# Streaming-encoder trunk on one core: families, merge gates and output projection issue each product as two of 256 columns

## What is computed

```python
mod = silu(c) @ ada_w + ada_b                 # shift, scale, gate
h = rms_norm(x, norm_w) * (1 + scale) + shift # 4096 x 1024
p = h @ w_in                                  # the families below
gq, gk, gv, gz, glr, hq, hf, hi, hz, mg = split(p)
o_g = gated linear attention (gq, gk, gv, decay from glr), normed, * silu(gz)
o_h = HGRN2 recurrence (hq, hf, hi), normed, * silu(hz)
g_a, g_b = split(sigmoid(mg + merge_b))       # merge gates
m = g_a * (o_g @ w_up_gla) + g_b * (o_h @ w_up_hgrn)
out = rms_norm(x + gate * (m @ w_out), final_norm_w)
```

## Time and profile before

| | |
|---|---|
| median of 3 timed executions | 2898.24 us (2897.74 to 2898.29) |
| the profiled execution's own time | 2897.05 us |
| its span in the trace | 2895.3 us |
| TensorE busy | 2863.4 us, 14662 MATMULs, 14662 weight loads |
| VectorE busy | 1522.8 us |
| ScalarE busy | 1265.2 us |

### The profile page before, as it was taken

How to read it: one execution, slowest core, us unless ns; L and a number is a source line. 1 busy time by engine, 2 the same in 40 slices (tenths; PEclk the granted TensorE clock), 3 DMA queues, 4 the chain that set the end, 5 groups by cost and what they waited for, 6 DMA issues and landing times.

```text
span 2895.3 us, 38295 instructions
## 1 busy us (share of the span) xinstructions
PE 2863.4 (99%) x14662; PEld 2344.6 (81%) x14662; DVE 1522.8 (53%) x2004; ACT 1265.2 (44%) x1659; POOL 168.8 (6%) x295
## 2 busy tenths in 40 slices
PE   7999999999999999999999999999999999999998
PEld 4878888788887888888888888888888788887887
DVE  6555455544556445564554635546355463644644
ACT  3643336433463334633446433464335533355322
POOL 1010000100001000010000100001000010000100
PEclk9999999999999999999999999999999999999999
DMA  8223442233322343224432243322433224342232
GB/s 326 88 81 119 134 142 90 78 131 131 133 94 75 131 136 129 87 80 138 138 126 87 74 152 126 125 88 74 154 123 131 83 74 159 109 137 83 81 124 73
DMA packets 89950, 336.21 MB, mean 116 GB/s; under 512 B 9808, under 2 KB 10000, under 8 KB 88208
## 3 DMA queue, kind: packets, MB, share of 16 engines
q1 hardware_dynamic: 89744, 333.45, 34.8%
HBM read 316.63 MB, written 16.78 MB: 115 GB/s over the span
## 4 chain that ended last, share of the span: by engine, by line
PE 98%; DMA 1%; DVE 0%; ACT 0%; SPq 0%; POOL 0%; issue 0%; POOLq 0%; DVEq 0%; ACTq 0%
PE A L1024 46%; PE F L1035 33%; PE A L1084 12%; PE R L1120 1%; PE F L1147 1%; PE A L1162 1%; PE R L1203 1%; PE F L1141 1%; DMA ada_w<-in_ada 1%; PE R L1113 1%; PE R L1147 0%; PE R L1187 0%; PE R L1186 0%; PE R L1162 0%; PE R L971 0%; PE A L982 0%
## 5 line engine op out<-in xcount | busy, mean ns | idle before, releaser
L662 DVE TENSOR_TENSOR w_lo<-w_raw,w_hi 128x1024 fp32r<-128x1024 f32 (+1 forms) x480 | 588.4, 1226 | 1059.9 <-ACT w_hi L451 1056.3
L451 ACT ACTIVATE w_hi<-w_raw 128x1024 fp32r<-128x1024 f32 (+1 forms) x480 | 507.4, 1057 | 752.8 <-PE A L1024 479.8
L1024 PE MATMUL A<-w_hi,h_hi 128*128 128x512 f32 (+1 forms) x1536 | 582.5, 379 | 0.1
L1024 PE MATMUL A<-w_lo,h_hi 128*128 128x512 f32 (+1 forms) x1536 | 572.9, 373 | 0.0
L1024 PE MATMUL A<-w_hi,h_lo 128*128 128x512 f32 (+1 forms) x1536 | 572.6, 373 | 0.0
L1035 PE MATMUL F<-h_hi,w_hi 128*128 128x512 f32 x1408 | 553.9, 393 | 0.0
L1035 PE MATMUL F<-h_lo,w_hi 128*128 128x512 f32 x1408 | 548.3, 389 | 0.0
L1035 PE MATMUL F<-h_hi,w_lo 128*128 128x512 f32 x1408 | 548.2, 389 | 0.0
L1024 PEld LDWEIGHTS A<-w_hi,h_hi 128*128 128x128 f32 x1536 | 288.3, 188 | 61.2 <-issue 9.4
L1024 PEld LDWEIGHTS A<-w_hi,h_lo 128*128 128x128 f32 x1536 | 288.5, 188 | 51.5
L1024 PEld LDWEIGHTS A<-w_lo,h_hi 128*128 128x128 f32 x1536 | 288.6, 188 | 47.5 <-issue 0.2
(11 more groups left out here) (188 smaller groups left out, 2832.3 us busy)
## 6 DMA issues: line engine op xcount, KB each, us to landing
w_raw<-in_w_stream SPq DMA_DIRECT2D x464, 512.0 KB, 3.5
xy<-in_x SPq DMA_DIRECT2D x8, 2048.0 KB, 8.6
result<-xy SPq DMA_DIRECT2D x32, 512.0 KB, 3.5
xf<-in_xt SPq DMA_DIRECT2D x30, 512.0 KB, 4.3
xn<-in_x SPq DMA_DIRECT2D x28, 512.0 KB, 5.1
ada_w<-in_ada SPq DMA_DIRECT2D x12, 1024.0 KB, 19.9
w_raw<-in_w_stream SPq DMA_DIRECT2D x16, 544.0 KB, 6.0
xy<-in_x SPq DMA_DIRECT2D x4, 512.0 KB, 13.8
```

Source lines behind the costliest of these rows:

```text
L451: AF(w_hi[:, s % RING, 0:n], w_raw[:, s % RAW, 0:n], ACT.Copy).then_inc(w_hi_done.sem, 1)
L662: V.tensor_tensor(w_lo[:, s % RING, 0:n], w_raw[:, s % RAW, 0:n], w_hi[:, s % RING, 0:n].bitcast(fp32), ALU.subtract).then_inc(w_split.sem, 1)
L1024: last = mm(A[t][:, 0:width], src[ia][:, k, t * P:(t + 1) * P], w_[iw][:, s % RING, kk * width:(kk + 1) * width], start=(k == 0 and n == 0 ...
```

## The change

Wherever `token_major` has a width of 512, and in all of `feature_major`, the products run over columns 0 to 255 first and then over columns 256 to 511, with the loop over the halves outside the loop over the pieces. Each half repeats all weight loads. Only the very first product of a bank has the start flag. The 272-column products, the up projection and the hosted products stay as they are.

```diff
                 for t in range(NT):
                     if part == 0:
                         pe.wait_ge(free.sem, free.at(b, free_n[t]))
-                    for kk in range(k_per):
-                        k = part * k_per + kk
-                        for n, (ia, iw) in enumerate(PASSES):
-                            last = mm(A[t][:, 0:width], src[ia][:, k, t * P:(t + 1) * P],
-                                      w_[iw][:, s % RING, kk * width:(kk + 1) * width],
-                                      start=(k == 0 and n == 0), stop=(k == KT - 1 and n == 2))
+                    for c0, c1_ in ((0, 256), (256, 512)) if width == 512 else ((0, width),):
+                        for kk in range(k_per):
+                            k = part * k_per + kk
+                            for n, (ia, iw) in enumerate(PASSES):
+                                last = mm(A[t][:, c0:c1_], src[ia][:, k, t * P:(t + 1) * P],
+                                          w_[iw][:, s % RING, kk * width + c0:kk * width + c1_],
+                                          start=(k == 0 and n == 0 and c0 == 0), stop=(k == KT - 1 and n == 2),
+                                          skip_group_check=True)
...
             def feature_major(b, s, dst):
-                for k in range(KT):
-                    for n, (iw, ia) in enumerate(PASSES):
-                        last = mm(dst[:, :], w_[iw][:, s % RING, k * P:(k + 1) * P], h_[ia][:, k, :],
-                                  start=(k == 0 and n == 0), stop=(k == KT - 1 and n == 2))
+                for fr in (slice(0, 256), slice(256, 512)):
+                    for k in range(KT):
+                        for n, (iw, ia) in enumerate(PASSES):
+                            last = mm(dst[:, fr], w_[iw][:, s % RING, k * P:(k + 1) * P], h_[ia][:, k, fr],
+                                      start=(k == 0 and n == 0 and fr.start == 0), stop=(k == KT - 1 and n == 2),
+                                      skip_group_check=True)
                 last.then_inc(slot_done.sem, 1)
```

## The result

The changed kernel takes 3032.6 us (median of 4, 3029.4 to 3035.2) against 2898.3 (2897.7 to 2898.9): a ratio of 1.046, 95% interval 1.0445 to 1.0481, 134 us slower. The forecast was slower, 2980 us with a range of 2950 to 3035, so the direction and the range held, and the likeliest value was 53 us short.

What follows compares the result with a forecast made beforehand. The prediction took TensorE to bound the kernel: 2897.05 us for the profiled execution plus 80 for slower split products made 2977, 2978 with the median's 1.2 above the profiled run, rounded up to 2980, range 2950 to 3035.

Steps and rivals of the forecast that it cites:

- What bounds the kernel: Whole kernel: TensorE bounds it, 98% of the chain, so longer products go straight into the time.
- the 1820 forecast: Weight loads: 9600 added at 0.19 us each would raise their busy time by about 1820 us.
- Why a product of 256 columns costs more than half: Split products: a 128-column load, 0.11 us, nearly fills its 0.114 us cover, so load and stream touch.
- The rival of the load that hides whole: Split products: each added load hides under its predecessor's 256 columns; 2898 to 2907 us, chance 0.12.
- The 24 us estimated from it: Split products: by the skill's columns over 2.4 GHz plus 2.5 ns, the split adds 24 us, giving 2922.
- (a): Split products take the tri products' pace, 117.5 ns: 8.3 ns more for each of 9600, 80 us.
- addresses as what could make it wrong: Split products: pace may differ between token_major and feature_major or between passes, unseen in tri rows; no size given.
- The rival of the fixed cost: Split products: a fixed cost each whatever the width, 119.3 ns at 256 columns; 114 us, 3012 us, chance 0.25.
- 256 columns no faster than 272: Split products: the load sets 126.0 ns, so two cost 252.0; 243 us more, 3141 us, chance 0.05.
- The rest, costed at nothing: Slot starts, semaphores, queued work on ScalarE and VectorE, and adding up in one bank: no added time.
- The rival on the fetching of instructions: TensorE's 400 split slots: a stall of some 0.1 us each adds 40 us, about 3020 us, chance 0.03.

Runs made afterwards that it cites:

- e1: Changed kernel with feature_major put back whole, so only token_major's 512-column products are split: 2979.1 us, ratio 1.028.
- e2: Changed kernel with token_major put back whole, so only feature_major's products are split: 2953.1 us, ratio 1.019.
- e8: Changed kernel with feature_major loading only 64 of 128 columns of each weight piece, leaving out half the rows: 2976.5 us in one execution.
- e12: Changed kernel with w_hi and w_lo moved 64 bytes on in memory, nothing else different: 2971.9 us, ratio 1.0252.
- e11: Kernel before plus eleven runs of 48 products, loaded or moving piece of h shifted in memory: 117.9 to 120 ns at 256 columns; total time not given.
- e7: Kernel before plus ten runs of 48 products ahead of tri, varying operands and widths: 113.3 to 120 ns at 256 columns; total time not given.
- e5: Changed kernel with the products split at column 384 instead of 256: 3485.9 us, ratio 1.203.
- e3: Changed kernel with slot 59, the last of each block, left whole: 3017.3 us, ratio 1.0411.
- e10: Kernel before plus ten other runs of 48 products, with fixed or changing weights and 64 or 96 loaded columns; total time not given.
- e13: Kernel before, products whole, with w_hi and w_lo moved 64 bytes on in memory: 2944.2 us, ratio 1.016.
- e9: Kernel before with only slot 59, the last of each block, split: 2913.2 us, ratio 1.0054.

## Why the prediction was right, and where it was off

*What bounds the kernel.* Right. 9600 products were split (e1 and e2 add up to the change), and what each got longer went straight into the time. The weight loads' records, added up, rose from 2643 to 4524 us, near the 1820 forecast, but that isn't what a page calls busy: there overlapping loads are merged, and the rise is 515 us.

*Why a product of 256 columns costs more than half.* The mechanism held, in part. With half the load it runs at 113.4 ns (e8), which is the half of 226.7, and the cost is then nothing; with the whole load it is 120.0. But a load as long as its cover isn't enough by itself: in e12 the whole load of 128 columns costs nothing in the merge gates (113.4), so the cost takes the long load and this placement together. The rival of the load that hides whole is refuted for these operands where they lie, and comes true in that other placement for part of the slots. What goes on between load and stream at a multiple of 256 bytes no run shows. The Trainium skill ("TensorE: Matmul & The Clock Gate", section "Back-to-back issue gap"), which the prediction set beside this rival, gives its columns over 2.4 GHz plus 2.5 ns for a product by itself and not for a stream of them. The 24 us estimated from it compare with 128 here.

*The value taken, (a), 117.5 ns.* This is the term that was mis-sized: 120.0 ns, so 128 us in place of 80. "Because width, loaded columns and type are the same" was not enough. `tri` lies 192 bytes off a multiple of 256 and the pieces of the change on one, and e11 gives 117.9 and 120.0 for just this difference. The prediction named addresses as what could make it wrong, and took no other value for it.

*The rival of the fixed cost* gave 119.3 ns and 3012 us, closer than my own value. As a number it holds from 256 to 512 columns (120.0, 146.7, 173.3, 226.7). As a mechanism it fails: half a load brings 113.4 at 256 columns (e8), and below that stands a floor of 112 ns (e7) which took e5 to 3486 us.

*256 columns no faster than 272.* Refuted, 120 against 126.

*"The rest, costed at nothing."* The starts of slots were right to within 0.06 us each. What was missing is the loop's branch, some 10 us. The rival on the fetching of instructions put a stall at each of 400 slots; it sits at 6 places, 1.6 to 2.0 us beyond a product's pace each. I had looked at how fast instructions are issued and not at what covers the fetch behind a branch.

*The sum as it came out:* 2898 + 128 + 10 + 2 - 7 = 3031, for 3032.6 measured. The 2 is the up projection.

What stays open: why 320 and 384 columns take their length plus 13.3 ns whether 64 or 128 columns are loaded, why 512 columns take 230.0 with 64 loaded and 226.7 with 128, what picks 113.3 or 117.8 ns where load and stream aren't a multiple of 256 bytes apart, and why 512 columns are slower there.

## What to carry to other kernels

Where a weight load is nearly as long as the product that covers it, halving the columns need not be free even though stream and load both fit: here 6.7 ns for each product of 256 columns, and 4.6% of the whole with the gaps. A price taken from another product of the same shape was 2% off here and made a third of the loss go missing, since the place of the operands in memory moves it (113 to 120 ns at the same width). And the products at the end of TensorE's loop are what covers the fetch behind the branch: with the last slot left whole (e3) what was left of each gap is 0.26 us or nothing. Keep long instructions last.

## What the runs showed of the hardware that was not expected

- Load and stream together depend on where they lie to one another in memory: 120.0 ns for 256 columns at a multiple of 256 bytes (e7, e10, e11 and the change), 117.9 or 113.3 at 64 or 192 bytes (e7, e11, e12); but 512 columns are best at the multiple, 226.7 against 228.8 (e11) to 233.3 ns (e13).
- A run settles: behind hosted work the first products of the changed kernel vary (113 to 125 ns) and then lock to one pace for the rest of the slot.
- Products with a load of 128 columns come no faster than 111 to 112 ns apart, whether 128 or 192 columns are streamed (e7); with 64 loaded they take 60 and 88.5 (e10).
- Where the fetch for the loop's branch leaves a gap, the first product starts 1.7 to 1.9 us after the landing (after, e3, e9).
